# Recurrent stage: the x tile of a block moved one block ahead, between the two groups of gate matmuls

## The reference

```python
xc = _centred_depthwise_conv(x_rnn, conv_w[l], conv_b[l])          # width 4
r = jax.nn.sigmoid(jnp.einsum('bsni,dnij->bsdnj', xb, wa) + ba)     # xb = xc in 10 blocks of 128
i = jax.nn.sigmoid(jnp.einsum('bsni,dnij->bsdnj', xb, wx) + bx)     # d: forward, backward
log_a = -LRU_C * r * jax.nn.softplus(-lam)
a = jnp.exp(log_a)
u = jnp.sqrt(-jnp.expm1(2.0 * log_a)) * (i * x32[:, :, None, :])
h_fwd = _linear_scan(a[:, :, 0], u[:, :, 0], reverse=False)
h_bwd = _linear_scan(a[:, :, 1], u[:, :, 1], reverse=True)
rnn = (h_fwd + h_bwd) * jax.nn.silu(g_rnn)
merged = (jax.nn.sigmoid(m_attn) * (attn @ w_branch_attn[l])
          + jax.nn.sigmoid(m_rnn) * (rnn @ w_branch_rnn[l]))
out = merged @ w_out[l] + b_out[l]
x = _layernorm(ALPHA * x + out, ln_gain[l], ln_bias[l])
```

## Time and profile before

| | us |
|---|---|
| median of 3 runs | 1138.46 |
| lowest, highest | 1138.01, 1139.72 |
| span of the profiled execution | 1137.3 |
| recurrent stage, from the gates of block 0 to the merge loop | 402.75 to 881.16 |

### The profile page before, as it was taken

How to read it: one execution, slowest core, us unless ns; L and a number is a source line. 1 busy time by engine, 2 the same in 40 slices (tenths; PEclk the granted TensorE clock), 3 DMA queues, 4 the chain that set the end, 5 groups by cost and what they waited for, 6 DMA issues and landing times.

```text
span 1137.3 us, 13279 instructions
## 1 busy us (share of the span) xinstructions
PE 1087.7 (96%) x4810; PEld 880.6 (77%) x4810; DVE 677.6 (60%) x797; ACT 397.9 (35%) x526; POOL 386.0 (34%) x198
## 2 busy tenths in 40 slices
PE   8999999999999999999889899898899999999996
PEld 6888788888788888878668677686688878788885
DVE  6567877006777637377585685785773542334575
ACT  3134333113333463735545446355441111111012
POOL 4221221322221325275144243342323454543223
PEclk9999999999999999999899999999999999999999
DMA  7110110331100112221011010110121252322502
GB/s 271 55 38 19 37 30 27 134 107 38 38 22 24 56 65 93 84 75 47 28 56 47 28 55 28 44 57 9 55 74 37 74 184 74 111 74 95 220 37 111
DMA packets 22517, 78.46 MB, mean 69 GB/s; under 512 B 2512, under 2 KB 2768, under 8 KB 22352
## 3 DMA queue, kind: packets, MB, share of 16 engines
q1 hardware_dynamic: 19888, 69.48, 18.6%
q10 hardware_dynamic: 2592, 8.48, 1.9%
HBM read 65.36 MB, written 12.58 MB: 69 GB/s over the span
## 4 chain that ended last, share of the span: by engine, by line
PE 68%; DVE 18%; issue 5%; ACT 3%; DMA 3%; POOL 1%; SPq 1%; DVEq 0%; ACTq 0%; POOLq 0%
PE proj L477 16%; PE proj L480 16%; PE proj L483 16%; DVE state L970 4%; DVE state L1196 3%; DVE conv L973 3%; PE aux L477 2%; PE aux L480 2%; PE aux L483 2%; PE aux L539 2%; DMA raw<-stream 2%; PE aux L521 1%; PE proj L698 1%; PE aux L698 1%; PE proj L697 1%
## 5 line engine op out<-in xcount | busy, mean ns | idle before, releaser
L477 PE MATMUL proj<-xt_hi,w_hi 128*128 128x512 f32 x896 | 362.4, 404 | 4.9 <-DVE xt_lo L970 2.5
L480 PE MATMUL proj<-xt_lo,w_hi 128*128 128x512 f32 x896 | 356.1, 397 | 0.0
L390 POOL TENSOR_SCALAR w_hi<-raw 128x1024 fp32r<-128x1024 f32 (+1 forms) x74 | 85.4, 1154 | 646.2 <-PE proj L477 609.2
L483 PE MATMUL proj<-xt_hi,w_lo 128*128 128x512 f32 x896 | 282.7, 397 | 0.0
L393 POOL TENSOR_TENSOR w_lo<-raw,w_hi 128x1024 fp32r<-128x1024 f32 (+1 forms) x74 | 209.7, 2833 | 6.2
L477 PEld LDWEIGHTS proj<-xt_hi,w_hi 128*128 128x128 f32 x896 | 169.5, 189 | 42.6 <-issue 4.7
L483 PEld LDWEIGHTS proj<-xt_hi,w_lo 128*128 128x128 f32 x896 | 169.5, 189 | 41.0
L480 PEld LDWEIGHTS proj<-xt_lo,w_hi 128*128 128x128 f32 x896 | 169.7, 189 | 35.1
L970 DVE TENSOR_TENSOR racc<-proj,racc 128x1024 f32<-128x1024 f32 x40 | 49.0, 1224 | 85.0 <-PE proj L483 85.0
L780 ACT ACTIVATE probs<-masked,neg_max 128x385 f32<-128x385 f32 (+1 forms) x64 | 38.0, 593 | 136.5 <-DVE neg_max L1064 136.5
L477 PE MATMUL proj<-h_hi,w_hi 128*128 128x512 f32 x160 | 63.6, 398 | 0.0
(11 more groups left out here) (139 smaller groups left out, 1716.9 us busy)
## 6 DMA issues: line engine op xcount, KB each, us to landing
raw<-stream SPq DMA_DIRECT2D x81, 512.0 KB, 3.5
spill<-part ACTq DMA_DIRECT2D x16, 512.0 KB, 2.6
attn_in<-spill SPq DMA_DIRECT2D x8, 1024.0 KB, 5.1
x_raw<-x_t SPq DMA_DIRECT2D x8, 512.0 KB, 9.2
rows<-x_rows SPq DMA_DIRECT2D x8, 512.0 KB, 8.0
out<-rows SPq DMA_DIRECT2D x7, 512.0 KB, 2.6
raw<-stream SPq DMA_DIRECT2D x10, 256.0 KB, 2.6
rotary<-tables SPq DMA_DIRECT2D x1, 1024.0 KB, 12.5
```

Source lines behind the costliest of these rows:

```text
L390: nc.gpsimd.tensor_scalar(hi, raw[:, raw_slot, cols], 1.0, 0.0, ALU.mult, ALU.add)\
L477: i = nc.tensor.matmul(banks[:, h * HALF:(h + 1) * HALF], wh, mov_hi[:, h * HALF:(h + 1) * HALF], start=first, stop=False)
L480: nc.tensor.matmul(banks[:, h * HALF:(h + 1) * HALF], wh, mov_lo[:, h * HALF:(h + 1) * HALF], start=False, stop=False)
L483: i = nc.tensor.matmul(banks[:, h * HALF:(h + 1) * HALF], wl, mov_hi[:, h * HALF:(h + 1) * HALF], start=False, stop=last)
```

## The change

It does four things. The tile x of block b+1 is computed in pass b, between `gates(b, 0)` and `gates(b, 1)`. The tile g of block b+1 comes last in pass b, and the branch tiles of pass b use buffers 1, 0, 1, 0. The stream, SP and POOL take the units in the new order: gate weights, x, branch, g. ACT and DVE have new programs: ACT takes the sigmoids of the second gates after the square roots, and `finish_block(b)` and `silu_gate(b+1)` end pass b; DVE forms one less decay squared first, puts adds between the steps, and has the taps and `conv_lo` of block b+1 before and between the scans of block b. The loops over blocks are written out. The first adds of `racc` are copies, and POOL's zeroing of it goes. Of blocks 2 to 9:

```diff
 PE
-                        tile(u, j, f, 0)
-                        tile(u + 1, 1 - j, f, 1)
-                        gates(u + 2, b_index, 0)
-                        if j == 0:
-                            pe.wait_ge(rnn_split, b_index + 1)
-                        rnn_branch(u + 3, j, f + 1, i, (0,))
-                        gates(u + 2, b_index, 1)
-                        rnn_branch(u + 3, j, f + 1, i, (1, 2, 3))
+            for b in range(RNN_BLOCKS):
+                u, f = gates_unit(b), FILL_X0 + 1 + 3 * b
+                gates(u, b, 0)
+                if b < RNN_BLOCKS - 1:
+                    next_tile(u + 1, f, 0)
+                gates(u, b, 1)
...
+                if b % 2 == 0:
+                    pe.wait_ge(rnn_split, b + 1)
+                last_one = b == RNN_BLOCKS - 1
+                branch = u + (1 if last_one else 2)
+                rnn_branch(branch, ring_number(branch) % 2, (f, f) if last_one else (f + 1, f),
+                           (b // 2 - 1) % 2, 0 if last_one else 1)
+                if last_one:
+                    next_tile(UNIT_C, FILL_C, 0)
+                    next_tile(UNIT_C + 1, FILL_C, 1)
+                else:
+                    next_tile(u + 3, f + 2, 1)
 POOL
-            nc.gpsimd.memset(racc[:, :, :], 0.0).then_inc(racc_zero, 1)
...
+            for b in range(RNN_BLOCKS):
+                unit = gates_unit(b)
+                gate_weights(unit, unit % 2, b or None)
+                for n in range(1, ring_units(b) + 1):
+                    ring(unit + n, number, (unit + n) % 2, number % 2)
+                    number += 1
 ACT
-                        pad_x(b, f)
-                        conv_begin(b, f)
-                        finish_block(b - 1, 1 - i if j else i, 1 - j)
-                        conv_high(b)
-                        silu_gate(b, f)
-                        recurrence(b, lambda n: None)
+            for b in range(RNN_BLOCKS):
+                f = FILL_X0 + 1 + 3 * b
+                sigmoids(b, 0)
+                decays(b)
+                if b < RNN_BLOCKS - 1:
+                    pad_x(b + 1, f)
+                roots(b)
+                sigmoids(b, 1)
+                if b < 2:
+                    for n in range(2):
+                        spill_branch(N_GROUPS - 1, 4 * b + n, 1 - n, f + n)
+                if b < RNN_BLOCKS - 1:
+                    conv_begin(b + 1, f)
...
+                if b < RNN_BLOCKS - 1:
+                    conv_high(b + 1)
+                finish_block(b, b // 2 % 2, b % 2)
+                if b < RNN_BLOCKS - 1:
+                    silu_gate(b + 1, f + 2)
 DVE
-                        block_head(b, f, 1 - i if j else i, 1 - j)
-                        recurrence(b, lambda n: add_branch(4 * j + n, f + 1 + n // 2))
+                one_less_decay(b)
+                add(0)
+                gated_input(b)
+                add(1)
+                scan_input(b)
+                add(2)
+                if not last_one:
+                    for tap in range(1, CONV_W):
+                        conv_tap(b + 1, tap)
+                add(3)
+                scan(b, 0)
+                if not last_one:
+                    conv_low(b + 1)
+                scan(b, 1).then_inc(scanned, 1)
+                gated_sum(b)
+                finish_block(b, b // 2 % 2, b % 2)
+                if not last_one:
+                    silu_gate(b + 1, f + 2)
```

More of the change, by code:

```diff
@@ L67, with columns_b, place @@
 COLS_B = UNIT_B * UNIT
-COLS_P = COLS_B + sum(WIDTHS_FIRST)
-COLS_PAIR = sum(WIDTHS_PAIR)
-COLS_C = COLS_P + (PAIRS - 1) * COLS_PAIR
+def columns_b():
+    at, found = COLS_B - 2 * UNIT, {}
+    def place(name, width):
+        nonlocal at
+        found[name] = (at, width)
+        at += width
+    for p in range(PAIRS):
+        for j in range(2):
+            b = 2 * p + j
+            place(("x", b), UNIT)
+            place(("g", b), UNIT)
+            place(("gates", b), HALF)
+            if p == 0:
+                place(("attn", 2 * b), UNIT)
+                place(("attn", 2 * b + 1), UNIT)
+            else:
+                place(("rnn", p - 1, j), UNIT)
+    place(("merge", 0), UNIT)
+    place(("merge", 1), UNIT)
+    return found, at - 2 * UNIT
+COLS, COLS_C = columns_b()
 FILLS_GROUP = HEADS + 1 + 4
 FILL_X0 = N_GROUPS * FILLS_GROUP - 4
[L75 to L78, removed]
+FILL_C = FILL_X0 + 3 * RNN_BLOCKS
 FILL_D = FILL_C + 5 + KT - 1
@@ L305, in encoder_layer, with gates_unit, ring_units, ring_number @@
         halves = [slice(0, HALF), slice(HALF, D_MODEL)]
+        def gates_unit(b):
+            return UNIT_B + 5 * b if b < 2 else UNIT_P + 4 * (b - 2)
+        def ring_units(b):
+            return 4 if b < 2 else 3
+        def ring_number(unit):
+            before = [b for b in range(RNN_BLOCKS) if gates_unit(b) < unit]
+            return unit - len(before)
         block = ctx.enter_context(nc.Block())
@@ L329, in _ @@
                     load(i * 2 + n, n, i * (2 * UNIT) + n * UNIT)
[L330 to L338, removed]
+            for b in range(RNN_BLOCKS):
+                rest = [("attn", 2 * b), ("attn", 2 * b + 1)] if b < 2 else [("rnn", b // 2 - 1, b % 2)]
+                if b < RNN_BLOCKS - 1:
+                    rest = [("x", b + 1)] + rest + [("g", b + 1)]
+                for n, name in enumerate([("gates", b)] + rest):
+                    unit = gates_unit(b) + n
+                    load(unit, unit % 2, *COLS[name])
             for n in range(2):
@@ L646, in rnn_branch, with next_tile @@
                     last.then_inc(filled[b], 1)
[L648 to L656, removed]
+            def next_tile(unit, fill, b):
+                tile(unit, ring_number(unit) % 2, fill, b)
             pe.wait_ge(scores_masked, N_HEADS * NB + 1)
```

192 lines of the change are left out of this document (79 added, 113 removed).

## The result

The changed kernel takes 1150.6 us (median of 4 runs, 1147.44 to 1152.11), the kernel before 1138.24: a ratio of 1.0103 [1.0089, 1.0116]. It is slower, as forecast, but by 12.4 us where the sum said 29.5. The profiled execution of after took 1147.44 us, its span 1145.6, so 8.3 more than the span of before. This is the fastest of the four runs; I compare the spans.

The account below looks back on a forecast made before the run. PE, busy 96% of the span, was taken as the bound. Blocks 0 and 1 -1.8, block 2 -2.5, blocks 3 to 8 +19.1, block 9 and tail +13.1, clock +1.6: +29.5, 1168.0 us, range 1148 to 1188.

Parts of the forecast that it names:

- the ring: Blocks 3 to 8: ACT and DVE closed over `h_lo`, with POOL's collisions, give 48.0 us a block, +19.1 for the six.
- PE's side: All blocks: no product added, `conv_lo` wait covered by 25 us; blocks 0 and 1 -1.8 us, block 2 -2.5.
- The closed ring: ACT cannot begin block b+1 before `h_lo` of b: ACT 19.9 plus DVE 22.0 make 41.9 us, over PE's 39.4.
- POOL on that ring: POOL's weight splits hold up DVE instructions with two SBUF inputs: 6.8 us of collisions a block, bounds 0 to 12.1.
- The walk of one block: Step-by-step timing of one block from its first gate matmul: collisions 0.9, 1.1, 1.7, 0.9 and 2.2, next gates at 48.0.
- The lower clock: PE after its idles in blocks 3 to 8: would cost twice 1.6 us a block, costed at nothing as covered by later waits.
- PE's idles: Each of blocks 3 to 8: 4.4 us for `pad_x`, 3.4 for the second add, 0.5 for the third, 0.3 for `conv_lo`.
- Block 9 and the tail: PE waits 6.2 for sigmoids, 4.0 and 3.9 for adds, 0.5 for the next tile: +13.1 us, plus 1.6 of lower clock.
- (a): Rival, lighter collisions: two of 2.03 us a block, period 46.0, total +17.5, 1156 us; chance 0.14.
- (b): Rival, the ring meets no split: period 41.9, -8.3 us in all, 1130 us, deciding at a period of 43.1; chance 0.06.
- (c): Rival, PE's clock stays low longer: 51.2 us a block, +19.2 more, 1187 us; chance 0.18 together with heavier collisions.
- (d): Rival, PE never waits and all 39.8 us return: 1099 us, needing ACT to begin block b+1 before `h_lo`; chance 0.04.

Follow-up runs that it names:

- e1: Changed kernel with POOL splitting only the first 64 columns of each unit in the recurrent stage (output not the reference's): 1125.48 us, 41.14 a block.
- e3: Changed kernel with ACT's first sigmoids and tanh of block b+1 put ahead of `finish_block` of block b: 1130.80 us, 41.88 a block.
- e4: Changed kernel with ACT's `pad_x(b + 1)` moved between the two squares: 1149.02 us, 44.72 a block.
- g1: Changed kernel with one more ACT copy, 1.06 us, before `h_hi` in blocks 2 to 8: 1159.79 us, 46.19 a block.
- g2: Changed kernel with one more PE product, 1.4 us, before the g tile of blocks 2 to 8: 1142.90 us, 43.76 a block.
- f4: e3 plus, in block 9, two branch tiles between the gate groups and DVE's adds of these ahead of its `one_less_decay`: 1124.68 us.
- e2: Kernel before with most of POOL's splitting in the recurrent stage left out (output not the reference's): 1098.20 us, ratio 0.9651.
- f3: f2 plus a POOL wait holding the branch unit's split until DVE's taps of that block, all work done: 1103.07 us, ratio 0.9695.
- f2: Kernel before with loads and splits reordered to x, gate weights, g, branch, PE's order of work kept: 1124.00 us, ratio 0.9875.

## Why the prediction was right, and where it was wrong

Slower was forecast for the ring: +19.1 us in blocks 3 to 8. These came out 1.6 faster, and the kernel is slower by its end alone. So the direction came true, but not for the main reason that was given.

*PE's side.* Right. `conv_lo` no longer holds the gates; blocks 0 and 1 gave the 1.8 us, block 2 2.2 for the 2.5 forecast.

*The closed ring.* Right, and the best of the prediction: the sum of rows gave 41.9, e1 measured 41.14. The bare ring follows the edits: 38.9 where e3 opens it, 40.1 where e4 takes `pad_x` out of it, 42.2 or 42.9 where g1 adds a copy, 41.2 where g2 adds to PE alone.

*POOL on that ring.* This is the step that failed. The walk of one block charged 6.8 us of collisions; the runs show 3.1, between 2.3 and 3.9 in single turns. With it, 48.0 a block came out as 44.55. The rule by which it walked held in the pairs shown here: the instruction that began first kept the other back. The Trainium skill (SBUF — State Buffer, Who interferes with whom) says the same, that the order of issue decides who blocks, and that a Vector instruction with at most one SBUF input, outside its two-port modes, is left alone; this trace agrees (`h_lo` at 726.90, 0.13 behind a w_lo, took 3.35; the add from PSUM at 670.82 ran beside a w_lo in 1.21). What was wrong were the phases, read to a tenth of a us from a sum of forty durations. The prediction's five charges, one by one:
- the product behind the branch split, 0.9: not paid in the blocks shown. Where they met, at 724.99, the product had begun first (724.55) and POOL stood aside, 1.70 us for that w_hi.
- `h_lo` behind its w_lo, 1.1: 2.12 in the two long blocks; in the others it met the w_hi and paid 0.5 to 0.8.
- one less decay behind the g unit's w_lo, 1.7: not paid. The split came 2.2 us behind it (650.34 and 652.55), or its w_lo 0.19 behind it (739.98 and 740.17). The second is a near-tie that could as well have cost 2; in block 9 the product came behind the w_lo and took 3.10.
- the taps, 0.9 and 2.2: 0.65 in most blocks, 2.69 in the block of 678.75. Where they paid only 0.65, the scan paid 1.09 in their stead, which the walk did not have.

The walk also started from gates that begin at the end of `conv_lo`. In the 43.7 us blocks they began 2.3 us later (676.43 and 678.75), since PE had lost time earlier on. Splits are released by PE, so all of POOL came late against DVE, and missed it more often.

*The lower clock.* "Costed at nothing" was right as a price and wrong as to what it does. PE's idles and the first matmuls behind them, from the timeline of after:

```profile
566.66 0.51 PE L499 MATMUL proj<-h_hi,w_hi 128*128 128x512 f32 x1 [2.02 <-ACT padded L846]
...
663.05 0.50 PE L499 MATMUL proj<-h_hi,w_hi 128*128 128x512 f32 x1 [2.56 <-DVE racc L991]
...
706.74 0.50 PE L499 MATMUL proj<-h_hi,w_hi 128*128 128x512 f32 x1 [2.53 <-DVE racc L991]
...
819.05 0.80 PE L499 MATMUL aux<-conv_hi,gates_hi 128*128 128x512 f32 x1 [4.00 <-ACT decay L881]
...
833.25 0.50 PE L499 MATMUL proj<-h_hi,w_hi 128*128 128x512 f32 x1 [3.07 <-DVE racc L991]
```

Behind the 2.56 us at 663.05 the granted clock fell (0.96 in such blocks), behind the 2.53 at 706.74 it didn't (1.00 in 678.75 to 721.55). The length of the idle alone doesn't decide it: in g1 it fell behind 1.97 (0.93 in 682.19 to 728.98), and in e4 it stayed up behind 2.84 (1.00 in 723.22 to 768.10). The two rows, g1 and e4:

```profile
704.00 0.50 PE L499 MATMUL proj<-h_hi,w_hi 128*128 128x512 f32 x1 [1.97 <-ACT padded L846]
```

```profile
753.29 0.50 PE L499 MATMUL proj<-h_hi,w_hi 128*128 128x512 f32 x1 [2.84 <-DVE racc L991]
```

Back to after. Where it fell, PE ended its block later, and the split released by the g tile came 1.81 us behind the start of the taps (668.13 and 666.32) and cost 0.65 + 1.09. Where it didn't, the split came 0.93 behind (710.93 and 710.00) and cost 2.69, and the gates started only 0.5 us behind `conv_lo`, so that the next split met `h_lo` in full: the long block of 721.55. The slow clock hid under the ring, as the prediction had it, and it spared the ring some 1 us by making PE late. That a later PE can shorten the ring is shown by g2; that the clock does it in after is read from the rows and was not tried.

*PE's idles.* 4.4 for `pad_x` was forecast for each block and came as 2.0, twice; 3.4 for the add came as 3.4 or 2.5; none for `conv_lo`. They are shorter as the ring is shorter. Gate starts of 48 us and `h_lo` at 8 to 9 us in each block, two of the signs named, did not come; `h_lo` ended 5.5 us into most blocks.

*Block 9 and the tail.* The sum came out right by luck, +14.7 forecast and +14.1 measured; its terms were not. Idle time is 77.47 - 67.75 = 9.7 us for 14.6: the gates wait 4.0 for the sigmoids, not 6.2, since they start 2.3 us behind `conv_lo`, and `h_lo` meets no split there (1.23). The slow clock costs 67.75 - 61.9 = 5.9 us for 1.6: three idles over 2.6 us follow within 21 us, and the mean granted clock of the stretch is 0.91. The Trainium skill (TensorE: Matmul & The Clock Gate, A second HAM failure mode: psum-queue depth-cycling) warns of idles between groups of matmuls that wait for PSUM buffers; here, and only here, the trace agrees at a cost that matters. f4 takes 5.7 us back of what e3 has there.

*The rivals.* (a), 46.0 a block and 1156, was nearest: lighter collisions still, 44.55. (b) named 43.1 as the block at which faster turns to slower; e1, at 41.14, came out faster at 1125.5 for the 1130 worked out. (c), 51.2 a block: the clock did fall in five of the six blocks and the g tile did end behind `conv_lo`, but the block is 44.55, and g2 shows that a later PE doesn't lengthen it. (d), that ACT begins before `h_lo`, was ruled out by the program, and e3 is the kernel in which it may: 41.88 a block and 1130.8 us, not 1099. PE still idles 2.0 us a block, since the bare ring of 38.9 and its collisions are together longer than PE's 39.3.

*What was missed in the profile of before.* The prediction took the wait for `conv_lo` as a matter of PE's order and asked only what the new order does. That POOL made all of that wait (e2) stood in sight in the earlier trace rows, in the sum that took 3.25 us.

*Open.* Why runs of after lie between 1147 and 1152: the number of long blocks may differ from run to run, which one profile can't show. The memset of `racc` and the written-out loops were not tried alone; the windows leave them nothing beyond the 1.8 us of block 1. Whether a later release in f3 takes the last 0.33 us a block was not tried.

## What to carry to other kernels

When an edit takes away the wait of the busiest engine, go once around the programs of the others: a step that now waits for the end of the last block closes a ring, and here its bare length could be added up from rows within 2%. Before an order is rearranged to cover a late result, look at what makes it late: here one wait on GpSimd, placing its instructions where VectorE does not need two SBUF inputs, gave 2.3%, and with the gate weights first 3.1%. Collisions between two engines are decided by which starts first, so a walk through them gives a range and not a number: work out each near-tie both ways.

## What the runs showed of the hardware

- An added product on TensorE made the kernel 7.7 us faster (g2: 1.0038 [1.0026, 1.0051] for 1.0103 [1.0089, 1.0116]), with fewer collisions between GpSimd and VectorE.
- The granted clock stayed up after an idle of 2.53 us and fell after one of 2.56, in two neighbouring blocks of the same program. Over all runs it fell after 1.97 (g1) and stayed up after 2.84 (e4), and in f2 waits of 2.3 brought it down in every second block. What else decides was not looked for.
- The same split cost the same three taps 0.65 us in one block and 2.69 in another. Pairs began as close as 0.13 us (726.77 and 726.90: 2.12 us for VectorE) and 0.19 us the other way round (739.98 and 740.17: nothing for VectorE, 0.84 for GpSimd).
- A scan (2.28 alone, 3.37 behind a w_lo) is held up by GpSimd as an elementwise instruction is, and holds it up in turn (4.25 us for a w_lo in the earlier trace rows).
